# The first RMSNorm of a decoder trunk, reordered third by third: VectorE squares two of the thirds, the first weights are fetched ahead of the last third of x

## The reference, cut to what matters

```python
def rms_norm(x, w):
    xf = x.astype(jnp.float32)
    y = xf * lax.rsqrt(jnp.mean(xf * xf, axis=-1, keepdims=True) + EPS)
    return (y * w.astype(jnp.float32)).astype(x.dtype)
...
for i in range(DEPTH):
    hn = rms_norm(h, norm_mix_pre[i])
    if i % 2 == 0:
        m = deltanet_stickbreak_mixer(hn, hyb_w_in[j], ...)   # proj = u @ w_in comes first
```

## Time and profile before

| | |
|---|---|
| median of 3 runs | 2748.02 us (2747.98 to 2749.83) |
| span of the profiled execution | 2748.7 us |
| PE busy | 2678.9 us, 97% of the span |
| DVE, ACT, POOL busy | 46%, 23%, 37% |
| granted clock of TensorE, mean of the span | 0.99 of full speed |

### The profile page before, as it was taken

How to read it: one execution, slowest core, us unless ns; L and a number is a source line. 1 busy time by engine, 2 the same in 40 slices (tenths; PEclk the granted TensorE clock), 3 DMA queues, 4 the chain that set the end, 5 groups by cost and what they waited for, 6 DMA issues and landing times.

```text
span 2748.7 us, 44704 instructions
## 1 busy us (share of the span) xinstructions
PE 2678.9 (97%) x18073; PEld 2555.5 (93%) x18073; DVE 1266.2 (46%) x2119; ACT 626.3 (23%) x1108; POOL 1015.0 (37%) x462
## 2 busy tenths in 40 slices
PE   8999999999999999999999999899999999999998
PEld 7999788866999999999999989899899999999997
DVE  5666667566174444444442457612632222222235
ACT  4231333365151000000000342411420000000002
POOL 5444110034354444444333325052544444444440
PEclk9999999999999999999999999999999999999999
DMA  4236321110232222222223139641231111111112
GB/s 163 93 109 136 97 69 57 49 62 25 87 113 67 76 82 82 82 78 79 81 76 96 52 124 283 219 115 42 98 108 46 46 46 46 46 46 46 46 31 82
DMA packets 142550, 232.27 MB, mean 84 GB/s; under 512 B 34016, under 2 KB 104928, under 8 KB 140256
## 3 DMA queue, kind: packets, MB, share of 16 engines
q1 hardware_dynamic: 53552, 134.98, 15.9%
q10 hardware_dynamic: 88880, 95.59, 11.0%
HBM read 172.78 MB, written 61.96 MB: 85 GB/s over the span
## 4 chain that ended last, share of the span: by engine, by line
PE 89%; DVE 6%; ACT 2%; issue 2%; DMA 1%; POOL 0%; ACTq 0%; DVEq 0%; POOLq 0%
PE psum L806 25%; PE psum L807 24%; PE psum L808 24%; PE psum L892 2%; PE psum L1295 2%; PE psum L1269 1%; DVE area L2282 1%; DVE area L2249 1%; PE psum L1117 1%; DVE x_lo L2294 1%; PE psum L1282 1%; PE psum L1138 1%; PE psum L1387 1%; DMA resid<-area 1%; DVE area L2272 1%
## 5 line engine op out<-in xcount | busy, mean ns | idle before, releaser
L806 PE MATMUL psum<-x_hi,w_hi 128*128 128x344 f32 (+2 forms) x3456 | 1123.9, 325 | 0.7 <-issue 0.7
L807 PE MATMUL psum<-x_lo,w_hi 128*128 128x344 f32 (+2 forms) x3456 | 1105.5, 320 | 0.0
L808 PE MATMUL psum<-x_hi,w_lo 128*128 128x344 f32 (+2 forms) x3456 | 1104.9, 320 | 0.0
L764 POOL TENSOR_TENSOR w_hi<-stage,const 128x1024 fp32r<-128x1024 f32 x193 | 484.6, 2511 | 1515.0 <-PE psum L808 1346.5
L806 PEld LDWEIGHTS psum<-x_hi,w_hi 128*128 128x128 f32 x3456 | 650.0, 188 | 11.1 <-issue 3.7
L807 PEld LDWEIGHTS psum<-x_lo,w_hi 128*128 128x128 f32 x3456 | 650.0, 188 | 3.3 <-issue 1.7
L808 PEld LDWEIGHTS psum<-x_hi,w_lo 128*128 128x128 f32 x3456 | 649.4, 188 | 0.0
L767 POOL TENSOR_TENSOR w_lo<-stage,w_hi 128x1024 fp32r<-128x1024 f32 x193 | 486.3, 2520 | 15.1
L2754 DVE TENSOR_TENSOR area<-area,psum 128x344 f32<-128x344 f32 (+2 forms) x132 | 67.7, 513 | 653.4 <-ACT area L1971 653.4
L806 PE MATMUL psum<-act_hi,w_hi 128*128 128x344 f32 (+2 forms) x1056 | 341.6, 323 | 8.3 <-DVE area L2777 6.9
L808 PE MATMUL psum<-act_hi,w_lo 128*128 128x344 f32 (+2 forms) x1056 | 336.9, 319 | 0.0
(11 more groups left out here) (235 smaller groups left out, 2233.8 us busy)
## 6 DMA issues: line engine op xcount, KB each, us to landing
stage<-wstream SPq DMA_DIRECT2D x193, 512.0 KB, 3.5
s_set<-area ACTq DMA_DIRECT2D x8, 1600.0 KB, 7.1
proj<-area ACTq DMA_DIRECT2D x20, 520.0 KB, 2.7
area<-proj ACTq DMA_DIRECT2D x36, 256.0 KB, 3.7
resid<-area ACTq DMA_DIRECT2D x6, 1376.0 KB, 6.0
area<-resid ACTq DMA_DIRECT2D x6, 1376.0 KB, 11.4
area<-s SPq DMA_DIRECT2D x8, 1024.0 KB, 6.7
area<-proj ACTq DMA_DIRECT2D x12, 520.0 KB, 4.8
```

The costliest lines, as they stand in the source:

```text
L764: pool.tensor_tensor(per_block(w_hi[:, slot, :]), src, ones_block, ALU.mult).then_inc(high_split, 1)
L806: mm(out[:, 0:n], w_hi[:, slot, wk], hi[:, xk, a:a + n], start=first, stop=False)
L807: mm(out[:, 0:n], w_hi[:, slot, wk], lo[:, xk, a:a + n], start=False, stop=False)
L808: return mm(out[:, 0:n], w_lo[:, slot, wk], hi[:, xk, a:a + n], start=False, stop=last)
```

## The change

Four things move in the first norm:

- VectorE, not ScalarE, squares the second and the last third (4 instructions ahead of its first `norm_pre`); the sums of these thirds wait for a new semaphore, `first_square`. The squares of the last third lie in other memory, so they need not wait for the first sum.
- VectorE and ScalarE finish one third (scale, high, low) before the next. Before, ScalarE's and VectorE's steps of the first two thirds were interleaved.
- TensorE starts with 16 small products of constants, whose result nobody reads, then makes the sums of two thirds, the gates and `in_proj` 0 of the first third, and only then the sums of the last third and the other four groups.
- SyncE's queue loads the first two weight slabs between the second and the last third of x; the last third and the masks come behind them.

```diff
@@ SyncE
-            for c in (1, 2):
+            def load_first_x(c):
                 a, n = CUTS[c]
                 sp.dma_start(first_h[c][:, :, 0:n], xT[:, :, a:a + n]).then_inc(first_loaded[c], 16)
+            load_first_x(1)
+            for n, slot in ((0, 5), (1, 0)):
+                sp.wait_ge(split_done, n + 1)
+                sp.dma_start(stage[:, slot % 2, :], wstream[n]).then_inc(stage_loaded[slot % 2], 16)
+            load_first_x(2)
...
+                elif name == "gates":
+                    pass
+                elif name == "in_proj":
+                    load(0, js=range(1, 4))
+                    with sp.Fori(1, count) as i:
+                        load(i)
@@ TensorE
                     if c == 2:
                         pe.wait_ge(nm_normed, 2)
+                    if c:
+                        pe.wait_ge(first_square, 2 * c)
...
-            for c in range(3):
-                norm_sum(0, c, 1)
+            for _i in range(16):
+                mm(bank[5][:, 0:P], ones, ident, start=True, stop=True)
+            norm_sum(0, 0, 1)
+            norm_sum(0, 1, 1)
             pe.wait_ge(group_free, 6)
             first_group("gates", 3, 0)
+            first_group("in_proj", 0, 0)
+            norm_sum(0, 2, 1)
             first_group("gates", 4, 1)
-            first_group("in_proj", 0, 0)
             first_group("in_proj", 1, 1)
             first_group("gates", 5, 2)
             first_group("in_proj", 2, 2)
@@ ScalarE
-                if r == 0 and c == 2:
-                    act.wait_ge(nm_sum, 1)
...
             norm_square(0, 0, 1)
-            norm_square(0, 1, 1)
-            norm_root(0, 0, 1)
-            norm_square(0, 2, 1)
-            norm_root(0, 1, 1)
-            norm_high(0, 0)
-            norm_high(0, 1)
-            norm_root(0, 2, 1)
-            norm_high(0, 2)
+            for c in range(3):
+                norm_root(0, c, 1)
+                norm_high(0, c)
+            for _i in range(4):
+                act.sem_inc(nm_square, 1)
...
-                act.wait_ge(group_done, (1, 2, 5)[c])
+                act.wait_ge(group_done, (1, 3, 5)[c])
@@ VectorE
+            for c in (1, 2):
+                dve.wait_ge(first_loaded[c], 16)
+                n = CUTS[c][1]
+                for half in range(2):
+                    x = first_h[c][:, 4 * half:4 * half + 4, 0:n]
+                    V.tensor_tensor(first_sq[c][half][:, :, 0:n], x, x, mul).then_inc(first_square, 1)
             dve.wait_ge(params_loaded, 32)
-            norm_pre(0, 0)
-            norm_pre(0, 1)
-            norm_low(0, 0)
-            norm_low(0, 1)
-            norm_pre(0, 2)
-            norm_low(0, 2)
+            for c in range(3):
+                norm_pre(0, c)
+                norm_low(0, c)
```

More of the change, by code:

```diff
@@ L469, in trunk @@
         nm_square = sem("nm_square")
+        first_square = sem("first_square")
         nm_log = sem("nm_log")
@@ L536, in trunk @@
         sq_halves = halves_of(nv["sq"])
-        first_sq = [sq_halves, [carve(3 * T_ROWS + KT * 344, 4, 344), carve(A1 + 3 * KT * CW, 4, 344)], sq_halves]
+        first_sq = [sq_halves, [carve(3 * T_ROWS + KT * 344, 4, 344), carve(A1 + 3 * KT * CW, 4, 344)],
+                    [dn_result[i].rearrange("p h t -> p (h t)")[:, 0:4 * 344].rearrange("p (k t) -> p k t", k=4)
+                     for i in range(2)]]
         first_sums = [bank[7], bank[6], bank[7]]
@@ L888, in norm_sum @@
                 for k in range(planes):
-                    if k % 4 == 0 and not folded(r):
+                    if k % 4 == 0 and not folded(r) and (r or c == 0):
                         pe.wait_ge(nm_square, 2 * e + k // 4 + 1)
@@ L1488, in norm_square @@
                 x = first_h[c][:, :, 0:n] if r == 0 else nv["h"][c % 2][:, :, 0:n] if m else acc[:, :, a:a + n]
-                if r == 0 and c == 2:
-                    act.wait_ge(nm_sum, 1)
-                elif r:
+                if r:
                     act.wait_ge(nm_sum, e)
```

## The result

Over 21 runs of each kernel the median is 2754.47 us after and 2748.93 us before; the ratio is 1.0016, with a 95% interval of 1.0010 to 1.0022, which is 4.4 us (2.7 to 6.0) of 2748.93. The change costs time, a little less than the 0.2% named above; the forecast was 5.2 us. The profiled execution took 2754.84 us and spans 2753.1; in all runs on record the time is about 1.7 us longer than the span. So spans are compared with spans: 2753.1 against 2748.7, which is 4.4 us.

What follows compares the result with a forecast made beforehand. TensorE, busy 97% of the span, bounds the kernel, so its dense stretch's start sets the end. Starting 3.7 us later warm plus 1.5 for the clock gives 5.2 on the median 2748.0: 2753.2 us, range 2750.0 to 2757.0.

Steps and rivals of the forecast that it cites:

- the 0.2% named above: Smallest change of the whole kernel's time that a measurement can tell from none, 5.5 us; slower by more had chance 0.44.
- T0: Start of the first scaling in the first norm; put at 24.7 us, after four VectorE squares taking turns with GpSimd's splits.
- From T0 to the products and the group's end: First norm: first product can start at T0 + 3.45 us, first group ends at T0 + 8.0, before the clock's term.
- The order: TensorE's last third's sums, 4.47 us, move behind two groups; nothing saved in itself; 18.92 + 4.47 follow the first group.
- dense stretch: TensorE's full queue from the line 806 matmul, at 52.39 us before; a shift of its start was taken as the end's.
- the break-even of 21.0: The T0, in us, at which the new head would start the dense stretch at 52.39, as before.
- The clock: TensorE idles some 6.2 us before the first product, its clock falls to half; net 0.7 to 2.4 us, taken as 1.5.
- The sum: Whole kernel: 3.7 us warm loss plus 1.5 for the clock, 5.2 us later, 2753.2 us, +0.19%.
- B: Rival: last third of x lands after 19.6 us, costing one more turn; T0 27.1 or more, 2755.6 to 2758; chance 0.16.
- C: Rival: VectorE's squares do not collide with GpSimd's splits; T0 21.7, 2748.7 to 2750.5 us; chance 0.10.
- D: Rival: faster, the shift removes a later clock fall, at 561.00 us, returning up to 6.8 us; 2746.4 or 2743.3; chance 0.05.
- Edits at no cost: First norm: constant products, ScalarE's lost squares, second root and later low parts stay hidden behind other work and cost nothing.

Runs made afterwards that it cites:

- Experiment 2: Changed kernel, with GpSimd's first split waiting until all four VectorE squares are done; T0 20.96, dense stretch at 57.12 us, no ratio taken.
- experiment 5: Kernel before plus only the transfers' change: two first weight slabs loaded ahead of the last third of x; dense stretch at 49.90 us, ratio to before 0.9994.
- experiment 4: Changed kernel plus 24 more constant products in TensorE's idle time behind the second third's sums; dense stretch at 56.25 us, ratio to before 1.0037.
- experiment 1: Changed kernel with its two first weight slabs fetched behind the last third of x; T0 20.63, dense stretch at 54.82 us, ratio to before 1.0005.
- experiment 6: Kernel before with only TensorE's new order: last third's sums behind the first third's gates and in_proj groups; dense stretch 4.35 us later, no ratio taken.
- experiment 7: Changed kernel with the last third's sums again ahead of the first products, in their own PSUM bank; dense stretch at 53.61 us, ratio to before 1.0005.
- experiment 9: Changed kernel without the 16 constant products at its start; T0 24.59, dense stretch at 58.09 us, no ratio taken.
- experiment 8: Kernel before with only VectorE's squares of the second and last third ahead of its first scaling; T0 18.51, dense stretch at 50.59 us, no ratio taken.
- experiment 10: The kernel of experiment 11 without the 16 constant products; first scaling at 18.73, dense stretch at 50.48 us, no ratio taken.
- experiment 3: Changed kernel with VectorE squaring the last third behind the first third's low parts; T0 18.33, dense stretch at 51.62 us, ratio to before 0.9993.
- experiment 11: Changed kernel; ScalarE squares last third, in_proj split follows first low parts, last third's sums precede in_proj group; dense stretch at 49.37 us, ratio to before 0.9988.

## Why the prediction was right

**T0.** Forecast 24.7, measured 24.20. The mechanism was the one named: VectorE's four squares in front of its first scaling, in turns with GpSimd's splits. A pair of turns was put at 3.75, and the two squares that waited a whole turn took 3.74 and 3.73:

```profile
13.23 3.74 DVE L2330 TENSOR_TENSOR area<-area 128x1376 f32<-128x1376 f32 x1
...
20.55 3.73 DVE L2330 TENSOR_TENSOR dn_result<-area 128x1376 f32<-128x1376 f32 x1
```

The second split instruction held until the last third had landed, as forecast. Experiment 2 shows the turns (T0 20.96 without them) and experiment 5 that late x alone costs nothing. The Trainium skill (GPSIMD Engine Reference, Specifications) names instructions with two SBUF inputs as those that contend; this trace agrees, also where both inputs are the same tile. One reading for it was loose: the scaling of 3.95 us that the forecast took as "alone at first" had a split beside it from 35.82 on. The trace after has the clean case, 3.95 us for the same scaling at 31.96 with no split between 26.49 and 39.08, so the scaling is indeed not slowed.

**From T0 to the products and the group's end.** Forecast 3.45 and 8.0, measured 3.60 and 9.3 with the clock's fall, 8.1 without it (experiment 4). Here the sum was right for the changed kernel and would have been wrong for its neighbours: the low parts are themselves VectorE instructions with two SBUF inputs, and where a split ran beside them the way was 10.6 us (experiment 1) or more. In the changed kernel the second slab's split ended at 26.5, 1.6 us before the first low part. That was luck of the schedule, not something that I had checked.

**The order.** The sum had the right terms, 18.92 and 4.47 in front of the dense stretch, and "nothing is saved by that in itself" fell short of what it meant. In the kernel before those 4.47 us ran while the group had to wait for its low parts anyway; moved behind it they are paid in full. Experiments 6 and 7 give the order 4.35 us alone and 3.5 within the change. The two traces add up so: T0 5.23 us later, the way from T0 to the end of the first group 5.18 shorter (14.50 before, 9.32 after), the stretch behind it 4.67 longer (18.92 and 23.59), 4.72 in all. T0 was the visible part of the loss, and the break-even of 21.0 is what the order did: with the sums ahead again a T0 of 24.2 costs 1.2 us (53.61 − 52.39). The shorter way goes with the new order of VectorE and ScalarE, third by third, and with splits that are over earlier; no experiment changed the third-by-third order alone, so its share is not shown.

**The clock.** Forecast: idle 6.2 us, a fall, 1.5 us net. Measured: idle 5.9 us, 3.97 us of products at half clock, 1.2 us net (experiment 4 against the changed kernel, each from its own T0).

**The sum.** 5.2 forecast at the dense stretch, 4.72 measured; 4.4 by the ratio. No large errors cancel in it: T0 was put 0.5 us too late, the way with the clock at 9.5 for 9.3, the stretch behind it at 23.4 for 23.6. The median of the runs moved by 5.5 because it jumps between groups of runs that differ in their mean granted clock (21 runs after: 6 from 2749.8 to 2750.0 at 0.994, 4 from 2752.4 to 2752.9 at 0.993, 11 from 2754.5 to 2755.6 at 0.991 to 0.992). That the median fell into the last group was a matter of one run. Rivals B and C did not come: the last third was there at 18.05, 1.1 us before GpSimd's turn ended (19.18), and the squares collided. D's mechanism exists, and in the profiled execution it gave about as much as it took: the fall at 561.00 is absent after, others came.

**Edits at no cost.** Confirmed for the constant products as far as T0 goes (experiment 9); the 0.6 us by the clock there stay open. Confirmed for ScalarE's order: after 33.52 no group waits.

## What to carry to other kernels

Work in front of the first product is free as long as the product waits for something else; before moving it behind, ask what the waiting time will be filled with, since this one move cost 4.4 us. Moving elementwise work onto VectorE and starting GpSimd earlier can each be harmless or a gain (1.8 and 2.5 us earlier at the dense stretch here, one profile each, the first of them with the odd event of the last section) and still cost together, when both engines then have instructions with two SBUF inputs at the same time: lay the two timelines over each other, for the work that is moved and also for what follows it. And where a change moves a few microseconds at the start of a long kernel, measure it at a fixed instruction of the trace, not only by the run's time.

## What the runs showed of the hardware that was not expected

**Turns are not a law.** In experiment 8 one split instruction waited for four VectorE instructions in a row and took 8.27 us:

```profile
26.86 6.16 DVE L2299 TENSOR_TENSOR x_lo<-area,x_hi 128x1408 fp32r<-128x1408 f32 x4
```

```profile
27.01 8.27 POOL L770 TENSOR_TENSOR w_lo<-stage,w_hi 128x1024 fp32r<-128x1024 f32 x1
```

VectorE's four took 6.16 us, as if alone, which is why the low parts and with them the dense stretch came early. It is the only split of its kind in the 13 traces; GpSimd's request came 0.15 us behind VectorE's start. In the changed kernel a request 1.4 us behind VectorE's start got the next turn, and in this same run the two met again by turns (the split from 37.73 took 3.62 us). What decides it stays open.

**The rest of the time goes with the clock.** Span minus dense start, and the time at half clock between 60 and 2700 us, for profiled executions that share all the code behind the head:

| kernel | half clock, us | rest, us |
|---|---|---|
| experiment 1 | 17.1 | 2690.2 |
| experiment 10 | 20.5 | 2692.2 |
| experiment 9 | 23.9 | 2693.2 |
| experiments 3, 6, 8 | 27.3 | 2694.5, 2695.2, 2695.4 |
| after, and experiments 2, 7, 11 | 30.7 | 2696.0, 2695.9, 2696.1, 2696.6 |
| before | 34.1 | 2696.4 |
| experiments 5, 4 | 41.0 | 2699.4, 2702.8 |

From the first to the last line 23.9 us more at half clock go with 9.2 to 12.6 us more, somewhat less or more than half. It is not a law: experiments 5 and 4 have the same time at half clock and differ by 3.4 us. The runs of one kernel spread the same way: 2744.2 to 2752.8 us for the kernel before, and the 21 runs of the changed kernel lie in groups by their mean granted clock, as the section on the prediction lists them. The Trainium skill (TensorE: Matmul & The Clock Gate, What's actually happening) says that the clock's watch does not start with the kernel; that the falls differ from profile to profile at the same place in the code (in the stage near 561 us 13.7 us at half clock before, none after) agrees with it.
